# A two-layer decoder step: the samples' steps scale older rows first, most of the branches' combination joins their loop, and the first turn waits for one more projection tile

## The reference, cut to what matters

```python
a = p[:, :, 0] - lam * p[:, :, 1]                       # differential attention: two maps
oa = einsum('nhqk,nkhe->nqhe', a, v)
ob = gates[..., 0:1] * o_cmp + gates[..., 1:2] * o_sel + gates[..., 2:3] * o_win   # three branches
o = concatenate([rms_norm(oa, subln_w) * (1.0 - lam_init), ob])
return o @ w_out
```

## Time and profile before

| what | us |
|---|---|
| median of 3 runs | 2007.36 |
| lowest and highest of them | 2003.38, 2016.0 |
| the profiled execution, its own time | 2010.96 |
| its span, first to last instruction | 2009.3 |
| PE busy in that span | 1893.0 |
| DVE, ACT, POOL busy | 892.4, 470.5, 78.4 |

### The profile page before, as it was taken

How to read it: one execution, slowest core, us unless ns; L and a number is a source line. 1 busy time by engine, 2 the same in 40 slices (tenths; PEclk the granted TensorE clock), 3 DMA queues, 4 the chain that set the end, 5 groups by cost and what they waited for, 6 DMA issues and landing times.

```text
span 2009.3 us, 31177 instructions
## 1 busy us (share of the span) xinstructions
PE 1893.0 (94%) x13411; PEld 1693.8 (84%) x13411; DVE 892.4 (44%) x1652; ACT 470.5 (23%) x746; POOL 78.4 (4%) x146
## 2 busy tenths in 40 slices
PE   5989999999977899999999899999999899999998
PEld 3767778867746899999999787788879899999997
DVE  3433332254324563545453523265554754545452
ACT  1512221134443321111111332111123211111111
POOL 1000001400030000000000000000000000000000
PEclk7889999689897999999999999776759999999998
DMA  9567664500052212222223454120204222222211
GB/s 356 194 219 236 203 206 124 201 2 1 22 188 65 85 64 84 84 84 84 84 84 125 153 189 147 43 69 31 77 29 148 64 85 84 84 84 84 84 63 47
DMA packets 160173, 218.72 MB, mean 109 GB/s; under 512 B 7271, under 2 KB 131198, under 8 KB 159630
## 3 DMA queue, kind: packets, MB, share of 16 engines
q1 hardware_dynamic: 148814, 177.52, 26.7%
q0 software_dynamic: 11264, 39.86, 5.7%
HBM read 199.66 MB, written 21.76 MB: 110 GB/s over the span
## 4 chain that ended last, share of the span: by engine, by line
PE 90%; DVE 6%; ACT 2%; issue 1%; DMA 1%; SPq 0%; ACTq 0%; DVEq 0%
PE ps L1348 14%; PE ps L1346 13%; PE ps L1345 13%; PE ps L1034 4%; PE ps L1036 4%; PE ps L1035 4%; PE ps L1460 2%; PE ps L909 2%; PE ps L1136 2%; PE ps L1122 2%; PE ps L1311 2%; PE ps L1314 2%; PE ps L1312 2%; PE ps L960 1%; PE ps L1475 1%; PE ps L1078 1%
## 5 line engine op out<-in xcount | busy, mean ns | idle before, releaser
L1345 PE MATMUL ps<-arena_r,wring_r 128*128 128x288 f32 x2048 | 570.3, 293 | 7.4 <-DVE hbuf_r L2112 7.4
L1348 PE MATMUL ps<-arena_r,wring_r 128*128 128x288 f32 x2048 | 439.8, 296 | 0.0
L1345 PEld LDWEIGHTS ps<-arena_r,wring_r 128*128 128x128 f32 x2048 | 386.1, 189 | 7.7 <-issue 7.7
L1348 PEld LDWEIGHTS ps<-arena_r,wring_r 128*128 128x128 f32 x2048 | 328.7, 189 | 0.0
L1346 PE MATMUL ps<-hbuf_r,wring_r 128*128 128x288 f32 x1024 | 286.3, 295 | 0.0
L1346 PE MATMUL ps<-arena_r,wring_r 128*128 128x288 f32 x1024 | 284.5, 294 | 0.0
L1815 ACT ACTIVATE wring_r<-wring 128x2048 fp32r<-128x2048 f32 x64 | 122.5, 1917 | 618.5 <-DMA wring<-in_mlp_w 618.5
L1346 PEld LDWEIGHTS ps<-hbuf_r,wring_r 128*128 128x128 f32 x1024 | 193.9, 189 | 0.0
L1346 PEld LDWEIGHTS ps<-arena_r,wring_r 128*128 128x128 f32 x1024 | 192.4, 188 | 0.0
L2447 DVE SCALAR_TENSOR_TENSOR xbuf<-ps,mod,xbuf 128x288 f32<-128x288 f32 (+1 forms) x128 | 56.1, 480 | 245.5 <-PE ps L1348 245.5
L1034 PE MATMUL ps<-wring_r,xbuf_r 128*128 128x512 f32 x360 | 149.6, 415 | 0.0
(11 more groups left out here) (375 smaller groups left out, 2801.4 us busy)
## 6 DMA issues: line engine op xcount, KB each, us to landing
wring<-in_mlp_w SPq DMA_DIRECT2D x64, 1024.0 KB, 5.2
arena<-in_ada_w SPq DMA_DIRECT2D x40, 1024.0 KB, 5.8
wring<-in_even_w_in SPq DMA_DIRECT2D x14, 1024.0 KB, 7.8
wring<-in_gla_w_in SPq DMA_DIRECT2D x12, 1024.0 KB, 5.4
wring<-in_ada_w SPq DMA_DIRECT2D x4, 2048.0 KB, 28.0
xbuf<-xspill SPq DMA_DIRECT2D x2, 2304.0 KB, 8.8
arena<-in_cache_cmp_kv POOLq DMA_DIRECT2D x16, 256.0 KB, 10.1
wring<-in_cache_diff_k POOLq DMA_DIRECT2D x16, 256.0 KB, 3.1
```

The costliest lines, as they stand in the source:

```text
L1345: pe.matmul(bank, hi, x_hi[:, k, cols], start=k == 0, stop=False)
L1348: mm = pe.matmul(bank, lo, x_hi[:, k, cols], start=False, stop=k == KC - 1)
```

## The change

In PE's projection loop `turn(0)` is left out of pass 1 and done in pass 2, ahead of `turn(1)`; all later turns stay where they are. In DVE's loop over the samples' steps `so_scale(v-3)` and `so_keep(v-4)` move ahead of `s_max(v)` and `s_factor(v)`. The combination becomes a function of a range of samples, `s_combine(part)`: it is called in pass 17 for the first seven samples (24 instructions over 56 columns), and after the loop for the last one (24 instructions over 8 columns).

```diff
-                if u:
+                if u == 2:
+                    turn(0)
+                if u >= 2:
                     turn(u - 1)
...
+            def s_combine(part):
+
+                dve.wait_ge(so_kept, 2 * part.stop)
+                dve.wait_ge(gb_kept, 1)
+
+                def by_sequence_rows(rows):
+                    return rows.rearrange("p (n s) -> p n s", n=NS)[:, part, :]
+
+                for h in range(HA):
+                    dve.scalar_tensor_tensor(out=by_sequence_rows(hT[:, h, SEQ:T]), in0=osa[:, part, h, DS:2 * DS],
+                                             scalar=lam[:, 5:6], in1=osa[:, part, h, 0:DS], op0=ALU.mult, op1=ALU.add)
+                for h in range(HB):
...
+                    for b, x in enumerate(parts):
+                        ins = dve.tensor_tensor(x, x, by_sequence_rows(gb[:, 3 * h + b, :]), ALU.mult)
+                step(ins)
...
             for v in range(2 * NS + 4):
-                if v < 2 * NS:
-                    s_max(v)
-                    s_factor(v)
                 if 3 <= v <= 2 * NS + 2:
                     so_scale(v - 3)
                 if v >= 4:
                     so_keep(v - 4)
+                if v < 2 * NS:
+                    s_max(v)
+                    s_factor(v)
+                elif v == 2 * NS + 1:
+                    s_combine(slice(0, NS - 1))
                 if v in (15, 17):
                     rest_unit(W_OUT + v // 2 - 7, S_OUT0 + v // 2 - 7)
             step(dve.tensor_scalar(lam[:, 4:5], v2T[:, V2_SUB:V2_SUB + 1], 1.0 - LAM_INIT, None, ALU.mult))
-            dve.wait_ge(so_kept, 2 * NS)
-            dve.wait_ge(gb_kept, 1)
...
+            ins = s_combine(slice(NS - 1, NS))
             ins.then_inc(comb_ready, 1)
```

More of the change, by code:

```diff
@@ L2341, in so_keep @@
                                 ps[:, 7, 0:P].rearrange("p (s c) -> p s c", s=4)[:, :, 0:16]).then_inc(so_kept, 1)
+            def s_combine(part):
[7 more added lines that the diff above has]
+                for h in range(HB):
+                    g, r = h // 2, h % 2
+                    parts = [oc[:, g, :].rearrange("p (n r s) -> p n r s", n=NS, r=2)[:, part, r, :],
+                             osb[:, part, g, DS * r:DS * r + DS], osb[:, part, 2 + g, DS * r:DS * r + DS]]
+                    for b, x in enumerate(parts):
+                        ins = dve.tensor_tensor(x, x, by_sequence_rows(gb[:, 3 * h + b, :]), ALU.mult)
+                step(ins)
+                for h in range(HB):
+                    g, r = h // 2, h % 2
+                    ins = dve.tensor_tensor(osb[:, part, g, DS * r:DS * r + DS], osb[:, part, g, DS * r:DS * r + DS],
+                                            osb[:, part, 2 + g, DS * r:DS * r + DS], ALU.add)
+                step(ins)
+                for h in range(HB):
+                    g, r = h // 2, h % 2
+                    ins = dve.tensor_tensor(by_sequence_rows(hT[:, HA + h, SEQ:T]),
+                                            oc[:, g, :].rearrange("p (n r s) -> p n r s", n=NS, r=2)[:, part, r, :],
+                                            osb[:, part, g, DS * r:DS * r + DS], ALU.add)
+                return ins
             for v in range(2 * NS + 4):
-                if v < 2 * NS:
-                    s_max(v)
-                    s_factor(v)
                 if 3 <= v <= 2 * NS + 2:
```

## The result

The changed kernel took 1975.59 us in the median (1970.51 to 1982.33), the kernel before 2007.05 beside it (2003.38 to 2016.0): ratio 0.9842, 95% interval 0.9805 to 0.9879, that is 31.5 us faster. The forecast was 1981 with a range of 1972 to 1993. The profiled execution of the changed kernel took 1982.33 us, span 1980.7, against 2009.3: 28.6 us less. Lines of the code behind the turns have numbers higher by 2 than before: L1199 is L1201, L1233 is L1235, L2336 is L2338.

The account below looks back on a forecast made before the run. PE, busy for 94% of the span, was taken as the bound. Terms 8.0 + 18.8 + 1.4 - 1.6 = 26.6 us took 2007.4 to 1981 us, range 1972 to 1993.

Parts of the forecast that it names:

- The order in the loop: Samples' loop: the early scale ends PE's waits ahead of `s_values`, 18.8 us gained (15 to 19.3), passes of 3.34 us.
- the clock: Samples' loop: one of three stretches at clock 0.5 goes, 1.4 us gained (0 to 4.3).
- The first turn: Projection: PE's own work fills its 7.77 us wait ahead of `turn(0)`; 8.0 us gained (5.5 to 8.8).
- the wait for piece 2: Projection: the conditioning piece's load is issued earlier, so PE's 1.63 us wait for it goes.
- Two shorter waits (3.1 us in 4.1): Projection: PE waits 1.2 and 1.9 us ahead of the first two turns; may or may not keep the 2.5 us clock loss.
- Piece 3: Projection: this conditioning piece's load meets the 3968 KB copy; PE waits 0 to 2.5 us for it.
- The combination: End of the samples' loop: split in two, first part paid in full, last 1.9 us shorter; 1.6 us lost.
- PE's wait ahead of the output projection: Behind the samples' loop: PE's one wait there grows beyond 5.9 us, as DVE's tail is longer and PE ends sooner.
- ACT's copy: Rival, samples' loop: the copy in `s_keep_turn` holds `s_values`, only 3 us gained there; 1998 us, chance 0.10.
- the loads: Rival, samples' loop: loads of the cache become the bound, 3 us lost; 1984 us, chance 0.07.
- the projection's gain: Rival, projection: the gap fills again, leaving 2 of the 8 us; 1987 us, chance 0.12.
- the clock went up in the loop, not down: Rival, samples' loop: the clock stays low, at 0.5, making the kernel slower; 2015 us, chance 0.03.

Follow-up runs that it names:

- e2_order: The kernel before with only the scaling and keeping of older rows moved ahead of the maximum; 1987.27 us, ratio 0.9893.
- e7_both: The changed kernel with first turns one more tile later and samples 0 to 3 combined in pieces in passes 11 to 14; 1983.21 us, ratio 0.9883.
- e10_all: `e7_both` with GpSimd's 3968 KB memory-to-memory copy issued at 384 us, out of the projection; 1969.06 us, ratio 0.9817.
- e11_behind: `e10_all` with the 3968 KB copy issued behind the samples' combination instead; 1972.37 us, ratio 0.9825.
- e8_idle: The changed kernel with two idle DVE reductions over 1400 columns ahead of the scaling in passes 3 to 15; 2001.45 us against 2013.42.

## Why the prediction was right

**The order in the loop** was sized at 18.8 us and **the clock** at 1.4; together with the split's -1.6 that makes 18.6, and stage C gained 22.0. The waits went as forecast: 19.3 us became 2.2, the larger of them 1.8 us behind a low part of 2.28, which was foreseen at 0.5. A pass came out at 3.27 where 3.34 was worked out. The mis-sized term is the clock: "I take one of three, 1.4". All three stretches went, and the one that the rows show whole had cost 6.27 - 4.83 = 1.44 us, so some 4 us in the passes. The whole of stage C, before, in `e2_order` and in the changed kernel, shows more:

```profile
542.11:629.71 87.60, 62.74 (x848) 43.53 (x848) 26.40 (x91) 38.06 (x98) 15.65 (x28) 0.85 0.42 139
547.82:610.78 62.96, 55.83 (x848) 39.31 (x848) 26.43 (x91) 37.45 (x98) 15.70 (x28) 0.91 0.57 192
537.36:602.94 65.58, 56.19 (x848) 39.49 (x848) 28.58 (x115) 37.45 (x98) 15.69 (x28) 0.89 0.57 194
```

The new order alone took 24.6 us. Of these 17.7 are PE's idle time (24.86 to 7.13), where 18.8 were forecast, and 6.9 are busy time: the same 848 matmuls took 62.74 us before and 55.83 then. About 1 us of that, as an estimate, is not the clock: a pass without a wait came out 3.34 - 3.27 = 0.07 us shorter than the wait alone explains, and there were fourteen waits. The term rested on a stretch that was busy and slow; in the loop the runs show the clock to follow the waits.

**The first turn** was sized at 8.0 us (5.5 to 8.8). Over six profiles with this edit alone in the projection A is 247.3 in the mean, against 253.1 and 253.2 in two of the three with the old turns (255.1 in the third): 5.9 us. Two steps held: the wait for piece 2 is gone, and the first two turns wait 1.1 and 1.7 us. What the prediction left open, "Two shorter waits (3.1 us in 4.1) may keep that or not", came out against it: the clock fell to 0.50 behind them, the turn, fold and piece that take 129.70 - 127.84 = 1.86 us took 3.5, and tile 3 came 5.5 us earlier, not 7.2. Piece 3 cost PE 0.3 to 0.7 us in three of the six and nothing in the others.

**The combination** was sized at a loss of 1.6 us; it is 1.9 to 2.8, since the price of eight columns was taken too low. The place was right: DVE ends last there, nothing covers the first part. Over 56 columns an instruction took 3.63 / 24 = 0.151 us, where 0.148 was worked out, but over eight 2.42 / 24 = 0.101, not 0.079.

Here the Trainium skill's rule, weighed in the prediction (VectorE: DVE Perf Modes, "The TRN2 errata — SBUF-src ops pay a fixed extra latency per instruction"), can be read off. Twelve products take 1.00, 1.31, 1.60 and 1.71 us at 8, 32, 56 and 64 columns: (1.71 - 1.00) / 12 / 56 = 1.06 ns a column and 1.00 / 12 - 8 x 0.00106 = 0.075 us fixed, which as an estimate is 72 cycles at the 0.96 GHz that the Trainium skill gives there. The 58 cycles of the Trainium skill are near that for instructions in a row, its 150 are not.

**PE's wait ahead of the output projection** was forecast to become longer than 5.9 us. It is 4.5: PE spends 4.3 us earlier, ahead of the last `s_back`, where it stood 0.8 before. Together the two have grown from 6.7 to 8.8 us, so the longer tail of DVE is as forecast; its place was overlooked, since the row copy that the transpose needs stands on DVE behind the first part and the low part.

**The rivals.** ACT's copy fell to `e2_order`; the loads showed no wait at 274 GB/s; the projection's gain fell short by 2 us, not 6; the clock went up in the loop, not down. The copy that "runs on" in the projection costs the changed kernel 0.8 to 1.4 us of A at most, but 249.2 - 241.1 = 8.1 where the turns come later still (`e7_both` against `e10_all`).

The sum of the stage terms, 5.9 for A and 22.2 for C (the mean of 22.0 and 22.4), is 28.1 us where 26.6 was forecast. That it comes so near is in part luck: the first turn gave 2.1 us less, the waits 1.1 less and the split cost about 1 more, while the loop's clock gave some 4.5 to 5.5 more. The 28.1 lie between the two measured differences, 31.5 and 22; the spread between these fits that of D, 10.6 us between two profiles of the changed kernel, which the change doesn't touch.

A kernel that beats both is `e10_all` or `e11_behind`: later turns, the combination spread over passes with idle time, and the copy out of the projection; 34 to 37 us faster than before, where the changed kernel was 22 to 31.5. From L1062 to the end of the combination, where the edits lie, they are 4.4 to 4.7 us shorter than it; what the totals show beyond that lies in D and is not shown to be theirs.

## What to carry to other kernels

Put work whose inputs have long been ready ahead of work that waits for the same pass's results: here two steps moved ahead of two others, on an engine that was busy 44% of the span took 24.6 us from a loop of 87.6. Work moved "into the loop" is free only in passes where its engine waits; in the pass where the same engine ends last it costs its full length plus the fixed cost of the extra instructions. When a stage is made denser, look for transfers without a due time that share its window, and move those first.

## What the runs showed of the hardware that was not expected

Waits of 1.5 to 1.7 us in passes of 5 us were followed by stretches of TensorE's half clock, in all four profiles that had them, behind some of the waits of 1.5 us and behind each of the six of 1.7 ahead of a key pass in `e8_idle`. But being busy didn't bring it back in the prompt's attention: 0.71 over 60 us with PE busy for 58.6 of them, and the length of that stage fell on a few values (B of 183.4 three times to 0.1 us, all without the copy in the projection, and of 179.1 to 179.3 seven times, all with it).

A transfer that GpSimd asked for slowed those of SyncE: 1 MB landed in up to 21.1 us beside the 3968 KB copy (`e7_both`) and in 11.4 at most without it. The Trainium skill says the like: DMA: Bandwidth & Descriptors, "Issuing engines are not separate DMA queues", that transfers started by ScalarE, SyncE or GpSimd run on the same DMA engines and interleave. The runs agree.
